# The second block's convolution inputs projected first, and its taps spread over the projections and the scan's levels

## What is computed

```python
h = rms_norm(x, norm_mix_g)
c_a, c_g, q_r, f_r, i_r, g_r, gate_c, gate_r = split(h @ w_in)
# branch 1: convolution of 31 taps over time, by channel (512 channels)
u = c_a * sigmoid(c_g)
u = causal_depthwise_conv(u, conv_w, conv_b)          # 31 taps
y_conv = silu(layer_norm(u)) @ conv_w_out
# branch 2: gated linear recurrence, 4 heads of 128
f = lb + (1 - lb) * sigmoid(f_r);  q = silu(q_r);  k = 1 - f;  v = i_r
o = recurrence(q, k, v, log f)                        # decay by cumulated log f
y_rec = (rms_norm(o) * silu(g_r)) @ hgrn_w_out
x = x + (sigmoid(gate_c) * y_conv + sigmoid(gate_r) * y_rec) @ w_mix_out
# then cross attention to mem: k = rms_norm(mem) @ w_k, v = rms_norm(mem) @ w_v
# then 32 routed experts
```

## Time and profile before

| | us |
|---|---|
| runs shown, median of 3 | 1860.47 (1859.66 to 1860.87) |
| profiled execution, its own time | 1867.0 |
| span of that execution | 1865.0 |
| PE busy | 1653.0 (89%) |
| DVE busy | 850.3 (46%) |
| ACT busy | 540.4 (29%) |
| POOL busy | 340.4 (18%) |
| the stretch that the change touches | 990.7 to 1209.7 |

### The profile page before, as it was taken

One profiled execution on the slowest core, in us unless ns is written; L12 is line 12 of the kernel. 1 busy time (PEld: TensorE's weight loads), 2 busy tenths in 40 slices (PEclk: granted clock), 3 DMA queues, 4 the chain that ended last, 5 costly groups with the idle time before them and its releaser, 6 DMA issues.

```text
span 1865.0 us, 19658 instructions
## 1 busy us (share of the span) xinstructions
PE 1653.0 (89%) x7276; PEld 995.6 (53%) x7276; DVE 850.3 (46%) x1893; ACT 540.4 (29%) x1316; POOL 340.4 (18%) x338
## 2 busy tenths in 40 slices
PE   8898998887878878788878999999979999999997
PEld 5486677543333222222237999887754444444442
DVE  1787728668886555554552677721231011010111
ACT  2213512244343443434342573101121111111111
POOL 0000002244444434344310048000000000000000
PEclk9999989999989999999999999999989999999999
DMA  8671026899999999999973444443339999999993
GB/s 355 229 289 47 1 90 252 343 364 427 426 427 427 427 427 427 427 427 427 427 303 126 163 151 179 157 151 135 136 118 431 427 429 429 430 429 431 429 403 129
DMA packets 65452, 571.28 MB, mean 306 GB/s; under 512 B 7520, under 2 KB 7776, under 8 KB 8416
## 3 DMA queue, kind: packets, MB, share of 16 engines
q1 hardware_dynamic: 25344, 281.13, 37.2%
q0 software_dynamic: 39312, 286.28, 37.0%
q10 hardware_dynamic: 720, 2.89, 0.4%
HBM read 569.22 MB, written 1.05 MB: 306 GB/s over the span
## 4 chain that ended last, share of the span: by engine, by line
PE 65%; DMA 16%; DVE 9%; ACT 6%; issue 3%; another core or an unknown queue 1%; SPq 0%; DVEq 0%; ACTq 0%
PE bank L1264 18%; DMA big<-in_peer_dram,big 14%; PE bank L1002 11%; PE bank L1098 6%; PE bank L875 3%; PE bank L1281 3%; PE bank L1256 3%; PE bank L1020 3%; DVE big L361 2%; PE bank L879 2%; ACT big L627 2%; PE bank L978 2%; PE bank L1172 1%; PE bank L1081 1%; PE bank L1078 1%
## 5 line engine op out<-in xcount | busy, mean ns | idle before, releaser
L1002 PE MATMUL bank<-big 128*128 128x512 f32 x1024 | 500.7, 626 | 123.2 <-ACT big L627 122.8
L1002 PEld LDWEIGHTS bank<-big 128*128 128x128 f32 x1024 | 185.1, 194 | 433.0 <-ACT big L627 271.4
L475 POOL DMA_INDIRECT big<-in_peer_dram,big x256 | 268.0, 1047 | 548.3 <-PE bank L1002 361.7
L1550 DVE SCALAR_TENSOR_TENSOR big<-big,misc 128x1024 f32<-128x1024 f32 x128 | 156.9, 1226 | 131.8 <-DMA big<-in_peer_dram,big 128.7
L1550 DVE SCALAR_TENSOR_TENSOR misc<-big,misc 128x1024 f32<-128x1024 f32 x128 | 156.8, 1225 | 114.8 <-DMA big<-in_peer_dram,big 114.6
L1264 PE MATMUL bank<-big 128*64 128x512 f32 x768 | 168.0, 592 | 1.3 <-ACT big L790 1.3
L1821 DVE TENSOR_TENSOR big<-big,bank 128x512 f32<-128x512 f32 x16 | 11.0, 687 | 297.8 <-PE bank L1264 297.8
L621 ACT ACTIVATE big<-big 128x1 f32<-128x1 f32 x256 | 51.5, 201 | 327.4 <-DVE big L1550 165.7
L1264 PE MATMUL bank<-big,misc 128*64 128x512 f32 x512 | 113.4, 594 | 9.7 <-ACT big L790 9.2
L1264 PEld LDWEIGHTS bank<-big 128*64 128x64 f32 x768 | 65.5, 137 | 100.1 <-issue 100.1
L627 ACT ACTIVATE big<-const,big 128x128 f32<-128x128 f32 x256 | 102.7, 401 | 11.0 <-PE bank L1002 2.7
(11 more groups left out here) (360 smaller groups left out, 2205.4 us busy)
## 6 DMA issues: line engine op xcount, KB each, us to landing
big<-in_moe_down_dram SPq DMA_DIRECT2D x32, 2048.0 KB, 11.4
big<-in_moe_up_dram SPq DMA_DIRECT2D x32, 2048.0 KB, 15.0
ring<-in_second_dram SPq DMA_DIRECT2D x44, 1024.0 KB, 4.8
big<-in_moe_gate_dram SPq DMA_DIRECT2D x16, 2048.0 KB, 12.0
ring<-in_moe_gate_dram SPq DMA_DIRECT2D x16, 2048.0 KB, 12.3
ring<-in_first_dram SPq DMA_DIRECT2D x29, 1024.0 KB, 5.2
misc<-in_mod_rest_dram POOLq DMA_DIRECT2D x16, 1024.0 KB, 5.4
big<-in_peer_dram,big POOLq DMA_INDIRECT x256, 19.9
```

Source lines behind the costliest of these rows:

```text
L475: pool.indirect_dma_start(out=gathered[b % GATHERS], out_offset=None, in_=t["peer"], in_offset=bass.IndirectOffsetOnAxis(ap=rows[:, b:b + ...
L1002: last = nc.tensor.matmul(bank[2 * tt + half][:], diag[:, b % DIAGS, :], gathered[b % GATHERS][:, a:a + 512], start=(h == 0 and k == 0), s ...
L1550: dve.scalar_tensor_tensor(products[b % 2], gathered[b % GATHERS][:, 0:UNIT], 1.0, x_rows[:, b // PTOP % TT, :], ALU.mult, ALU.mult, accum ...
```

## The change

The order of units becomes ca, cg, f, q, i, g, gc, gr (all eight), xk, xv. The split units are now sixteen, g, gc and gr0 to gr3, none at levels 0 and 1, three at levels 2 to 5, two at 6 and 7. Levels 0 and 1 have two plain i units each; gr4 to gr7 are plain and stand behind the recurrence. `convolve` takes a range of steps, and DVE does its 93 in eleven pieces: 24 after `up`, 9 after kk, 9 after the scans, then 9, 9, 5, 5, 5, 5, 6, 7 at the levels. The zero fills and `h_lo` move ahead of them. The convolution's sums come right behind the recurrence on PE; all of xk and xv come after both normalisations' products.

```diff
-    for what, a, b in (("f", 0, 4), ("q", 0, 4), ("i", 0, 4), ("gr", 0, 4), ("ca", 0, 4), ("cg", 0, 4), ("g", 0, 4), ("gc", 0, 8),
-                       ("gr", 4, 8), ("xk", 0, 8), ("xv", 0, 8), ("ho", 0, 4), ("co", 0, 4), ("mix", 0, 8), ("xq", 0, 8), ("xo", 0, 8)):
+    for what, a, b in (("ca", 0, 4), ("cg", 0, 4), ("f", 0, 4), ("q", 0, 4), ("i", 0, 4), ("g", 0, 4), ("gc", 0, 8),
+                       ("gr", 0, 8), ("xk", 0, 8), ("xv", 0, 8), ("ho", 0, 4), ("co", 0, 4), ("mix", 0, 8), ("xq", 0, 8), ("xo", 0, 8)):
...
-BETWEEN = SECOND[SECOND.index(("ca", 0)):][:3 * (LEVELS + 1)]
+BETWEEN = SECOND[SECOND.index(("g", 0)):][:16]
+PARTS_AT = (0, 0, 3, 3, 3, 3, 2, 2)
+PARTS = [sum(PARTS_AT[:n]) for n in range(LEVELS + 2)]
+TAPS_EARLY = (24, 9, 9)
+TAPS_AT = (9, 9, 5, 5, 5, 5, 6, 7)
...
             for lev in range(LEVELS + 2):
...
-                if lev == 0:
-                    take2([("gr", 2), ("gr", 3)])
+                if lev in (1, 2):
+                    take2([("i", 2 * lev - 2), ("i", 2 * lev - 1)])
                 if lev >= 1:
+                    for m in range(PARTS[lev - 1], PARTS[lev]):
+                        take2(BETWEEN[m:m + 1])
+                        if m + 2 < len(BETWEEN):
+                            lead2(m + 2)
...
-            project([(w, i) for w in ("q", "i") for i in range(4)], Hv)
-            project([("gr", i) for i in range(4)], Hv)
+            project([(w, i) for w in ("cg", "f", "q") for i in range(4)], Hv)
...
-                if lev == 0:
+                if lev < 2:
+                    project([("i", 2 * lev), ("i", 2 * lev + 1)], Hv)
+                if lev == 2:
                     pe.wait_ge(S("h3_lo_ready"), 1)
                 if lev <= LEVELS:
-                    project_parts(range(3 * lev, 3 * lev + 3))
-            pe.wait_ge(S("memn_ready"), 1)
-            project([("xk", 0), ("xk", 1)], memn)
+                    project_parts(range(PARTS[lev], PARTS[lev + 1]))
...
+            dve.tensor_tensor(up[:, :, CONV_K - 1:], caT, sgate, ALU.mult).then_inc(S("up_ready"), 1)
...
+            some_taps(TAPS_EARLY[0])
...
             dve.tensor_scalar(kk, ff, -1.0, 1.0, ALU.mult, ALU.add).then_inc(S("kk_ready"), 1)
+            some_taps(TAPS_EARLY[1])
...
             link(ins)
+            some_taps(TAPS_EARLY[2])
...
-                rest2(3 * lev)
-                if lev == 4:
...
+                for m in range(PARTS[lev], PARTS[lev + 1])[:1]:
+                    rest2(m)
+                some_taps(TAPS_AT[lev])
...
-            convolve(dve, range(CONV_DVE), "taps")
```

More of the change, by code:

```diff
@@ L349, in first_done, with convolve @@
             eng.wait_ge(S("first_unit_done"), FIRST.index((what, i)) + 1)
[L351 to L362, removed]
+        def convolve(eng, tiles, taps, steps):
+            for s in steps:
+                j, n = s // len(tiles), s % len(tiles)
+                i = tiles[n]
+                w = v("conv_w", i * CONV_K + j)
+                if j == 0:
+                    ins = eng.tensor_scalar(cv[:, i, :], up[:, i, 0:T], w, v("conv_b", i), ALU.mult, ALU.add)
+                else:
+                    eng.wait_ge(S(taps), s - len(tiles) + 1)
+                    ins = eng.scalar_tensor_tensor(cv[:, i, :], up[:, i, j:j + T], w, cv[:, i, :], ALU.mult, ALU.add)
+                ins.then_inc(S(taps), 1)
         block = ctx.enter_context(nc.Block())
@@ L1099, in project @@
                     last.then_inc(S("second_unit_done"), 1)
-            project([("f", i) for i in range(4)], Hv, "H3_ready")
+            project([("ca", i) for i in range(4)], Hv, "H3_ready")
             pe.wait_ge(S("stdx_ready"), base("stdx_ready") + 2)
@@ L1146, in _ @@
                     last.then_inc(S("rec_ready"), 1)
-            project([("xk", 2), ("xk", 3)], memn)
+            pe.wait_ge(S("conv_ready"), 1)
+            for i in range(4):
+                last = nc.tensor.matmul(bank[4][:, 0:T], ones, cv[:, i, :], start=(i == 0), stop=(i == 3))
+            last.then_inc(S("meanc_ready"), 1)
+            project([("gr", i) for i in range(4, 8)], Hv)
+            pe.wait_ge(S("sqc_ready"), base("sqc_ready") + 1)
+            for i in range(4):
+                last = nc.tensor.matmul(bank[5][:, 0:T], ones, sqc[:, i, :], start=(i == 0), stop=(i == 3))
+            last.then_inc(S("varc_ready"), 1)
             for n in range(2):
                 pe.wait_ge(S("sqh_ready"), base("sqh_ready") + n + 1)
-                nc.tensor.matmul(bank[4 + n][:], ones, sqh[:, 2 * n:2 * n + 2, :].rearrange("p h t -> p (h t)"),
+                nc.tensor.matmul(bank[6 + n][:], ones, sqh[:, 2 * n:2 * n + 2, :].rearrange("p h t -> p (h t)"),
                                  start=True, stop=True).then_inc(S("ssh_ready"), 1)
[L1152 to L1164, removed]
+            pe.wait_ge(S("memn_ready"), 1)
+            project([(w, i) for w in ("xk", "xv") for i in range(8)], memn)
             for what, rhs in (("ho", och), ("co", cv)):
@@ L1599, in _, with some_taps @@
                 dve.scalar_tensor_tensor(Xv[:, k, :], Xv[:, k, :], v("final_norm_g", k), rsx[:, 0:T], ALU.mult, ALU.mult).then_inc(S("x2n_ready"), 1)
+            dve.memset(QE, 0.0)
+            dve.memset(KE, 0.0)
+            dve.memset(scT, 0.0)
+            dve.memset(up[:, :, 0:CONV_K - 1], 0.0)
+            dve.wait_ge(S("h3_hi_ready"), 1)
+            dve.tensor_tensor(h_lo, Hv, h_hi, ALU.subtract).then_inc(S("h3_lo_ready"), 1)
             dve.wait_ge(S("lb_ready"), 1)
             link(dve.tensor_scalar(lb1, lb, -1.0, 1.0, ALU.mult, ALU.add))
+            dve.wait_ge(S("taken2"), SECOND_ACT.index(("cg", 3)) + 1)
+            dve.tensor_tensor(up[:, :, CONV_K - 1:], caT, sgate, ALU.mult).then_inc(S("up_ready"), 1)
+            dve.wait_ge(S("up_ready"), 1)
+            taps_at = [0]
+            def some_taps(n):
+                convolve(dve, range(CONV_DVE), "taps", range(taps_at[0], taps_at[0] + n))
+                taps_at[0] += n
+            some_taps(TAPS_EARLY[0])
+            dve.wait_ge(S("taken2"), SECOND_ACT.index(("f", 3)) + 1)
             for i in range(4):
@@ L1661, in _ @@
                 if lev >= 1:
-                    rest2(3 * lev - 2)
+                    late = range(PARTS[lev - 1] + 1, PARTS[lev])
+                    for m in late[:1]:
+                        rest2(m)
                     take_level(lev - 1, masks[:, lev - 1, :])
-                    rest2(3 * lev - 1)
+                    for m in late[1:]:
+                        rest2(m)
                 dve.wait_ge(S("decay_ready"), lev + 1)
```

71 lines of the change are left out of this document (26 added, 45 removed).

## The result

| | before | after |
|---|---|---|
| median, us | 1860.58 (1859.66 to 1860.87) | 1879.22 (1878.77 to 1880.66) |
| ratio, with its 95% interval | | 1.0102 (1.0086 to 1.0118) |
| span of the profiled execution | 1865.0 | 1878.7 |
| from PE's first unit to the output projections | 219.1 | 236.4 |

The change costs 18.6 us, 1.0% of the time, the number of the forecast's sum. The row of the table that can be compared with it term by term is the last one: 1209.74 - 990.69 before, 1221.31 - 984.94 after, 17.3 us more.

A forecast was written before the change was run, and what follows sets the result against it. PE was taken as the bound, its wait ahead of level 0 as decisive; 4.6 + 17.1 + 2.4 + 0.6 + 1.4 - 7.5 = +18.6 us on the median 1860.5 gave 1879, range 1868 to 1887.

The forecast's parts named there:

- What bounds the kernel: Second block: PE has work almost throughout, so a change is won or lost by what PE waits for.
- The wait ahead of level 0: PE waits 18 us, not 0.98, for DVE's longer work ahead of level 0, with POOL alongside: +17.1 us.
- The prices of the walk: DVE's instruction times up to level 0 beside POOL: taps 0.61 us each, scans and gate taken at factor 1.5.
- The clock: Behind PE's wait at level 0 the granted clock drops to 0.50, slowing the next units: +2.4 us.
- Plain for split: On PE, eight more plain units at 3.46 us and eight fewer split ones at 2.88: +4.6 us.
- The later levels: Five to seven taps in each later level leave DVE 10.5 us against PE's 10.4, a dead heat: +0.6 us.
- The tail: No xk units left to hide DVE's taking of the last level ahead of the recurrence's products: +1.4 us.
- The prize: PE's waits at the convolution's two sums and the slow products behind them go with the taps moved: -7.5 us.
- no contention: Rival: POOL gives way to DVE ahead of level 0, wait 7.3 us, sum +7.5, 1868 us; chance 0.09.
- Heavier contention: Rival: 14 DVE instructions ahead of level 0 each wait for a whole POOL instruction, +11 us, 1890; chance 0.08.
- The covered wait: Rival: DVE has K and Q ready when PE reaches level 0, sum -2.2 us, 1858; chance 0.04.

The follow-up runs named there:

- e2: Changed kernel with PE's four i units ahead of level 0, gr4 to gr7 behind levels 0 and 1, xk0 to xk3 between the convolution's sums; 1864.4 us.
- e1: Changed kernel with POOL's taps held back until DVE has made level 0's K and Q products; 1880.5 us, ratio to before 1.0108.
- e3: Changed kernel with 72 unused products added on PE ahead of level 0, which kept PE busy for 31 us; 1889.4 us, ratio 1.0161.
- e3b: Changed kernel with 36 unused products added on PE ahead of level 0, to fill most of the wait; 1879.3 us, ratio 1.0108.
- e8: Changed kernel with e2's PE order, nine taps moved from ahead of level 0 as in e4, two xk units ahead of the recurrence's output; 1860.0 us.
- e7: e6 with zero fills and h_lo at the block's start and eight DVE taps ahead of taking the last level; 1852.3 us, ratio 0.9963.
- e5: Kernel before with only 11 of 31 taps on DVE's convolution tiles, the convolution left incomplete; 1854.9 us, ratio 0.9971, stretch 211.9 us.
- e6: Kernel before with DVE's convolution centring moved ahead of the recurrence's norm, taps left in place; 1855.4 us, ratio 0.9976.
- e4: Changed kernel with the nine taps between scans and level 0 moved behind the last level's last remainder; 1874.6 us, ratio 1.0082.

## Why the prediction was right

- **What bounds the kernel.** Right: PE, and the figure to watch was its wait ahead of level 0. e2 shows it most plainly, where filling the wait gives 13.9 us of the stretch back with DVE untouched.
- **The wait ahead of level 0**, +17.1: measured 17.43 - 0.98 = 16.5. Level 0 was forecast at 1070 and starts at 1063.27, which is 1069.0 counted from before's first unit. The split into DVE's work and POOL's contention was right too: 7.3 forecast for the walk alone, 7.17 in e1.
- **The prices of the walk.** A tap beside POOL 0.61, measured 0.62; memn 4.9, measured 5.1. Too high were the scans, 3.9 for 3.4, the opening three, 1.6 for 1.1, and kk, 1.0 for 0.8. The factor of 1.5 for what no row showed beside POOL was thus at the high end for the scans, 1.3, and right for the gate, 2.15 for 1.38. (The 88 taps of the earlier trace rows are those of the chain; DVE's timeline has 90 in 44.52 us, and the distance of 0.41 stands by either.)
- **The clock**, +2.4: 2.05, by after against e3. Its reason was half right. I took it from a wait of 6.85 us and argued that a longer one does as much; e3b shows that one of 1.93 us does nearly as much. And the 2.4 was one profile's number: the other ten give 1.8 to 3.1 behind the same wait.
- **Plain for split**, +4.6: no run changes this alone. The difference of e8 and e7 leaves 8.65 - 4.05 = 4.6 for it, and twelve plain units take 41.45 us in e2 (1004.62 to 1046.07), 3.45 each, as taken.
- **The later levels**, +0.6: the four from level 2 to 6 took 10.66, 10.52, 10.81 and 10.52 us, 0.8 above PE's own 10.42.
- **The tail**, +1.4: 1.51.
- **The prize**, -7.5: 7.9 in e5 behind the first four units, and no wait at the sums in after. Getting the taps out of the way does give it, as forecast. What the forecast missed is that 6.3 of it need no tap moved, only the recurrence's norm out of the centring's way (e6).

The terms measured sum to 16.5 + 2.05 + 4.6 + 0.8 + 1.5 - 7.9 = 17.6, against 17.7 of the stretch behind the first four units. So the forecast's sum was a microsecond high, and that the whole time moved by exactly its 18.6 is in part luck. In the two profiles the part behind the stretch is 2.1 us longer after than before, 1.7 of them in a stage that the change does not touch (below); whether the other executions have the missing microsecond there is not shown.

Of the rivals, no contention is out by the taps' rate in after and e1. Heavier contention, a whole POOL instruction of wait for each scan and gate, is out by their own rows: beside POOL eight scans took 0.8 us more than alone and the four gates 0.8 us more, 0.1 and 0.2 each and not 1.1. The covered wait was no part of this change. e8 makes it true and takes the tail's 1.4 away as well, which by the forecast's prices is -3.6; it stands at -0.5 behind the first four units. What the forecast of e8 lacked were the 4.05 us of the level from 2 to 3, which the sooner start brought beside POOL's work, some 1.4 of them by the clock.

## What to carry to other kernels

Work moved from behind a bottleneck's queue to ahead of a step that the bottleneck waits for costs its full length there, at the rate that it has beside whatever else it sets free; walk the engine's order from the last known time to that step before moving anything. Ask of a wait at the end of a long piece of work what stands directly ahead of the release: here 9.7 us of unrelated work, not the 44 us that caught the eye. And if an engine must wait, put work that depends on nothing late into the wait, rather than shorten it from the other side.

## What the runs showed that was not expected

The granted clock falls behind short waits, and not each time. The same wait of 2.96 us ahead of the query projections of the cross attention was free in the profile of before and cost 1.7 us in that of after, with the code there the same. PE's timeline, before:

```profile
1273.36 27.86 PE L1098 MATMUL bank<-H,ring 128*128 128x256 f32 x128 [2.96 <-DVE H L1717]
```

and after:

```profile
1284.92 29.55 PE L1094 MATMUL bank<-H,ring 128*128 128x256 f32 x128 [2.96 <-DVE H L1717]
```

It was free in e4 and e8 too, and cost the same 1.7 us in e1, e2, e3, e3b, e5, e6 and e7. Waits of 0.98 and 1.33 us left the clock at full rate in the earlier trace rows; one of 1.93 did not in e3b. One of 1.47 was followed by a granted clock of 0.50 in e8 (1088 to 1090) and by the full one in e4, at the same place of the code. What decides it between these was not settled.

Contention between DVE and POOL is nearly one-sided in after: DVE's taps go from 0.41 us apart to 0.62, while POOL's 61 instructions take 61.5 us beside them, less than the 68.4 they took beside the longer DVE instructions of the levels before. A step of two takes POOL 1.88 us beside the taps and 1.84 in before where DVE idles (1134.78 to 1136.62).
